# Starting one odd partial sum of a depthwise convolution on TensorE

## The chip, the cores and the metric
The kernel runs on one core of a Trainium2 chip. The metric is the device time in microseconds of one execution; the time given for a kernel is the median of its runs. The core has four engines that compute: TensorE (PE in the profile; PEld is its loading of weights), VectorE (DVE), ScalarE (ACT) and GpSimd (POOL). SyncE (SP) issues the loads. Each engine works through its own instructions in order, and engines meet only at semaphores.

## The reference
Three transformer-like blocks follow one another on 512 tokens of 1024 features. The change touches one place only, the convolution module of the second block:

```python
def conv_module(h, w_in, dw_w, dw_b, ln_g, ln_b, w_out):
    proj = h @ w_in                       # 1024 -> 3 * 2048
    a, b, z = jnp.split(proj, 3, axis=-1)
    u = a * jax.nn.sigmoid(b)
    c = depthwise causal convolution of u with dw_w (31 taps) + dw_b
    ...                                   # norm over 2048 channels, SiLU
    y = jax.nn.silu(cn).astype(h.dtype) * jax.nn.silu(z)
    return y @ w_out
```

For each of the 2048 channels, the output at a token is a sum of 31 taps, each a weight of that channel times `u` at one of the last 31 tokens.

## The kernel before
Features lie on the partitions and tokens along the free axis, so 128 channels by 512 tokens are one channel tile. The 2048 channels are done in eight pairs of channel tiles. A pair needs three weight tiles of 256 output features: its gate `b` (phase 0 or 3), its `a` (phase 1 or 4) and its `z` (phase 2 or 5). A round `i` has two pairs (`h` = 0 and 1, six phases `p`). Rounds 0 to 2 are the segment `seg`: round 0 is written out, rounds 1 and 2 are a loop. Round 3 (`LAST`) is the segment `last`. Below, pairs are counted from 0 to 7.

For every weight tile GpSimd splits the loaded 32-bit weights into a high part (L1406) and a low part (L1412), and TensorE makes 48 products (L1491): 8 blocks of the contraction (`k`), 2 channel tiles (`b`), 3 combinations of high and low parts, in the order k, b, combination. There are two slots for split weights and two accumulators, so the split of a tile waits until TensorE is through with the tile two before it.

The convolution of a pair goes like this:

- `sigmoid` (ScalarE, L2964) turns the accumulated gate into an SBUF tile, after TensorE has finished the gate tile.
- `glu` (VectorE, L2985 to L2988) copies the pair's weights to `wts` and multiplies `a` by the gate into `U`; `half_in` tells ScalarE of the first channel tile, `posted` tells of both.
- `act_products` (ScalarE): taps 6 and 7 begin the even and the odd sum of both channel tiles in PSUM (L2976, four instructions, counted by `begun`). Then taps 0 to 5 go to six SBUF buffers `PROD` (L2981, twelve instructions, counted by `products`).
- `add_half` (GpSimd, L3010) adds these six into `pool_sum`. It is called behind the splits of the next pair's gate and `a` tiles: two additions behind the first, three behind the second, and then `pool_done`. In round 3 the two halves of pair 6 stand behind the splits of phases 3 and 5.
- `conv` (VectorE, L3024): taps 8 to 30, for both channel tiles, each one `scalar_tensor_tensor` that adds a weighted, shifted view of `U` to the even or the odd sum. That is 46 instructions a pair. After each odd tap stands a drain, so that a sum is not read before it is written.
- `finish` (L3032, L3034) waits for `pool_done` and adds the three partial sums.

Pair 7 is done otherwise already, by `conv_last` (L3068): its odd taps 7, 9, 11 and 13 are TensorE's. ScalarE builds for each tap and channel tile a 128x128 diagonal of the weights (`products_last`, L3051), and `tensor_taps` (L3078) multiplies `U` by them within the `z` tile of pair 7, at k = 6. VectorE meanwhile does four even taps, each followed by a drain, and then waits for `tapped`.

Of the kernel before, what the change touches and what calls it, by code (L numbers as in the profile page):

```python
# [19 lines left out]
ACT = mybir.ActivationFunctionType  # L20
AX_X = mybir.AxisListType.X
ds = bass.ds

P = 128
S = 512
# [10 lines left out]
CONV_K = 31  # L36
# [2896 lines left out]
def conv_module_steps(nc, st, w, rhs, rescale):  # L2933


    ctx = ExitStack()
    products, half_in, begun, gate_free, pool_done, going, summed, diagonals_in, tapped = sems(
        nc, ctx, "dw", "products half_in begun gate_free pool_done going summed diagonals tapped")
    pad = CONV_K - 1
    U = st.spare[:, 0:3, :].rearrange("p c n -> p (c n)")[:, 0:2 * (S + 32)].rearrange("p (b n) -> p b n", b=2)  # L2940
    gate = st.spare[:, 3:5, :]
    sums = st.PS[:, 4:8, :]
    halfway = st.spare[:, 5:7, :]
    wts = st.spare[:, 9, 0:2 * CONV_K].rearrange("p (k b) -> p k b", b=2)
    pool_sum = st.spare[:, 10:12, :]

    PROD = (pool_sum, gate, st.spare[:, 12:14, :], st.spare[:, 14:16, :], st.extra[:, :, :], st.A[:, 14:16, :])
    BESIDE = len(PROD)
    LAST = 3
    DIAGONAL = range(BESIDE + 1, BESIDE + 9, 2)  # L2950
    diagonal = lambda b, n: st.spare[:, 7 + b, n * P:(n + 1) * P]
    ADDED = {0: 0, 1: 1, 3: 0, 5: 1}
    dw0 = st.col0["dw0"]
    weights = st.params[:, dw0:dw0 + 16 * CONV_K].rearrange("p (k c) -> p k c", c=16)

    def clear(e):

        for b in range(2):
            e.memset(U[:, b, 0:pad], 0.0)

    def sigmoid(e, acc, i, p):
        e.wait_ge(gate_free, i * 2 + (p // 3 + 1))
        e.sem_inc(going, 1)
        return e.activation(gate, acc, ACT.Sigmoid)  # L2964

    def silu(e, acc, i, p):
        return e.activation(st.A[:, ds(i * 4 + (16 + 2 * (p // 3)), 2), :], acc, ACT.Silu)

    def act_products(e, i, p, posted, begins=2):
        e.wait_ge(half_in, i * 2 + (p // 3 + 1))  # L2970
        for n in range(begins):
            for b in range(2):
                if n == 0 and b == 1:
                    e.wait_ge(*posted)
                k = BESIDE + n
                e.activation(sums[:, 2 * (k % 2) + b, :], U[:, b, k:k + S], ACT.Identity,  # L2976
                             bias=param(st, "conv_dw_b_2", i * 4 + (2 * (p // 3) + b)) if n == 0 else 0.0,
                             scale=wts[:, k, b:b + 1]).then_inc(begun, 1)
        for k in range(BESIDE):
            for b in range(2):  # L2980
                ins = e.activation(PROD[k][:, b, :], U[:, b, k:k + S], ACT.Copy, scale=wts[:, k, b:b + 1])  # L2981
            ins.then_inc(products, 1)

    def glu(e, acc, i, p):
        e.tensor_copy(wts, weights[:, :, ds(i * 4 + 2 * (p // 3), 2)])  # L2985
        e.tensor_tensor(U[:, 0, pad:pad + S], acc[:, 0, :], gate[:, 0, :], ALU.mult)
        e.drain().then_inc(half_in, 1)
        e.tensor_tensor(U[:, 1, pad:pad + S], acc[:, 1, :], gate[:, 1, :], ALU.mult)  # L2988
        return e.drain()

    def add_products(e, i, p):

        first = isinstance(i, int) and i == 0 and p < 3
        if first and p == 2:
            rescale(e)
        if first or p % 3 == 2 or isinstance(i, int) and i == LAST:
            return
        add_half(e, i * 2 + (p // 3 - 1), p % 3)

    def add_products_last(e, i, p):  # L3000

        if i == 0 and p in ADDED:
            add_half(e, 2 * LAST + (p // 3 - 1), ADDED[p])

    def add_half(e, pair, half):
        e.wait_ge(products, pair * BESIDE + (half + 1) * (BESIDE // 2))
        if half == 0:
            e.sem_inc(going, 1)
        for k in range(1, BESIDE // 2) if half == 0 else range(BESIDE // 2, BESIDE):
            ins = e.tensor_tensor(pool_sum, pool_sum, PROD[k], ALU.add)  # L3010
            if k == 1:
                ins.then_inc(gate_free, 1)
            e.drain()
        if half == 1:
            e.drain().then_inc(pool_done, 1)

    def conv(e, i, p):
        h = p // 3
        for k in range(BESIDE + 2, CONV_K):
            for b in range(2):  # L3020
                if k < BESIDE + 4:
                    e.wait_ge(begun, i * 8 + (4 * h + 2 * (k - BESIDE - 2) + b + 1))
                s = sums[:, 2 * (k % 2) + b, :]
                e.scalar_tensor_tensor(s, U[:, b, k:k + S], wts[:, k, b:b + 1], s, ALU.mult, ALU.add)  # L3024
            if k % 2:
                e.drain()  # L3026
        finish(e, i, h)

    def finish(e, i, h):
        e.drain()  # L3030
        e.wait_ge(pool_done, i * 2 + (h + 1))
        e.tensor_tensor(halfway, sums[:, 0:2, :], pool_sum, ALU.add)  # L3032
        e.drain()
        e.tensor_tensor(st.A[:, ds(i * 4 + 2 * h, 2), :], halfway, sums[:, 2:4, :], ALU.add).then_inc(summed, 2)  # L3034

    def phases(first, products_of, conv_of):
        after = lambda act: lambda e, acc, i, p: act(e, acc, i + first, p)
        of = []
        for h in range(2):
            c0 = (2 * first + h) * TW  # L3040
            of += [Phase(D_INNER + c0, act=after(sigmoid), order="gate"),
                   Phase(c0, dve=after(glu), takes=3 * h, more=conv_of, act_more=products_of),
                   Phase(2 * D_INNER + c0, act=after(silu))]
        return of

    def products_last(e, i, p):
        act_products(e, LAST, p, (last.posted, last.posted_at(i, p)), 2 if p < 3 else 1)
        if p < 3:
            for b in range(2):
                for n, k in enumerate(DIAGONAL):  # L3050
                    e.activation(diagonal(b, n), st.ident, ACT.Copy,  # L3051
                                 scale=weights[:, k, 14 + b:15 + b]).then_inc(diagonals_in, 1)

    def conv_last(e, i, p):
        h = p // 3
        if h == 0:
            return conv(e, LAST, p)
        even, odd = ([k for k in range(BESIDE + 2, CONV_K) if k % 2 == n and k not in DIAGONAL] for n in range(2))
        ahead = even[:len(even) - len(odd)]
        rest = [k for pair in zip(odd, even[len(ahead):]) for k in pair]  # L3060
        for at, k in enumerate(ahead + rest):
            for b in range(2):
                if at == 0:
                    e.wait_ge(begun, LAST * 8 + (4 + b + 1))
                if at == len(ahead):
                    e.wait_ge(tapped, b + 1)
                s = sums[:, 2 * (k % 2) + b, :]
                e.scalar_tensor_tensor(s, U[:, b, k:k + S], wts[:, k, b:b + 1], s, ALU.mult, ALU.add)  # L3068
            if at < len(ahead) or k % 2 == 0:
                e.drain()  # L3070
        finish(e, LAST, h)

    def tensor_taps(pe):
        pe.wait_ge(last.posted, last.posted_at(0, 4))
        pe.wait_ge(diagonals_in, 2 * len(DIAGONAL))
        for b in range(2):
            for n, k in enumerate(DIAGONAL):
                mm = pe.matmul(sums[:, 2 + b, :], diagonal(b, n), U[:, b, k:k + S],  # L3078
                               start=(n == 0), stop=(n == len(DIAGONAL) - 1))
            mm.then_inc(tapped, 1)  # L3080

    seg = Seg(w, rhs, LAST, phases(0, lambda e, i, p: act_products(e, i, p, (seg.posted, seg.posted_at(i, p))), conv),
              stride=2 * TW)
    seg.beside = add_products
    last = Seg(w, rhs, 1, phases(LAST, products_last, conv_last))
    last.beside = add_products_last
    last.first_sums = lambda e: add_half(e, 7, 0)
    last.last_sums = lambda e: add_half(e, 7, 1)
    clearing = Part(ctx)
    clearing.vector(clear)  # L3090
    clearing.gpsimd(lambda e: e.nop().then_inc(gate_free, 1))
    last.within = lambda pe, i, p, k: tensor_taps(pe) if (p, k) == (5, 6) else None
    last.chunk_ready = lambda c: (summed, c + 1)
    last.all_posted = lambda: (last.posted, last.posted_at(0, 4))
    return clearing, seg, last
# [614 lines left out]
```

## Time and profile before

| | |
|---|---|
| median of 3 runs | 2593.75 us (2593.53 to 2593.91) |
| the profiled execution, its own time | 2593.49 us |
| its span | 2590.4 us |
| granted TensorE clock, mean | 0.987 |
| busy share of the span | PE 97%, PEld 77%, POOL 60%, DVE 53%, ACT 26% |
| the convolution's pairs, first `glu` to last `finish` | 747.9 to 1039.8 us |
| L3024, instructions and busy time | 322, 220.3 us |
| L3010, instructions and busy time | 40, 95.9 us |

The profile is of one execution. Its span runs from its first to its last instruction, and its own time is 3.1 us longer. The shares are means over a kernel of many stages; what counts for the change is who waits for whom between 748 and 1040 us. The granted clock is TensorE's: 1.00 is 2.4 GHz and 0.50 is 1.2 GHz.

### The profile page before, as it was taken

The numbers are of one execution on the slowest core, as the hardware profiler recorded it, in microseconds if no ns is written. First come the engines' busy times: TensorE is split into PE (matmuls) and PEld (weight loads), VectorE is DVE, ScalarE is ACT, GpSimd is POOL, SyncE is SP. The second block draws the span as 40 slices with busy tenths as digits, with TensorE's granted clock in tenths as the row PEclk, the third lists the DMA queues.
The fourth block names the chain that finished last, engine by engine and source line by source line (L and its number), as shares of the span: only waits on it lengthen the run. The fifth ranks groups of instructions, "written<-read, shape, count | busy, mean of one in ns | idle before, by whom it ended". The sixth has DMA issues, their size and how long they took to land.

```text
span 2590.4 us, 30886 instructions
## 1 busy us (share of the span) xinstructions
PE 2514.1 (97%) x11112; PEld 1991.4 (77%) x11112; DVE 1361.2 (53%) x1915; ACT 668.8 (26%) x1102; POOL 1562.8 (60%) x1061
## 2 busy tenths in 40 slices
PE   7999999999999999999999998999999999999998
PEld 6885588888877776788867886767888777888885
DVE  5996652221379999968214426244356144534345
ACT  3006721100254434421022114133114121300002
POOL 2640257766779898567633765524764467666653
PEclk8999999999999999999999999999999999999999
DMA  9640123333222322133321222311332223223321
GB/s 298 222 157 1 33 67 96 97 98 98 98 82 82 97 81 66 54 98 98 97 81 33 97 84 67 95 50 52 100 93 66 66 81 95 69 96 97 97 80 55
DMA packets 224138, 231.42 MB, mean 89 GB/s; under 512 B 12219, under 2 KB 213788, under 8 KB 223900
## 3 DMA queue, kind: packets, MB, share of 16 engines
q1 hardware_dynamic: 221104, 229.33, 28.0%
q8 instruction: 65, 1.06, 0.2%
q10 hardware_dynamic: 2924, 0.66, 0.1%
q14 instruction: 45, 0.37, 0.0%
HBM read 227.87 MB, written 2.10 MB: 89 GB/s over the span
## 4 chain that ended last, share of the span: by engine, by line
PE 78%; DVE 11%; DVEq 5%; ACT 2%; issue 1%; POOLq 1%; DMA 1%; ACTq 0%; POOL 0%; SPq 0%
PE PS L1491 60%; PE PS L1438 5%; DVE PS L3024 3%; PE PS L1299 3%; DVE A L489 2%; PE PS L2084 1%; DVEq L491 1%; DVEq L3026 1%; PE PS L958 1%; PE PS L2286 1%; PE PS L2303 1%; DVE PS L3068 1%; PE PS L2075 1%; PE PS L2671 1%; DVE X L1066 1%
## 5 line engine op out<-in xcount | busy, mean ns | idle before, releaser
L1412 POOL TENSOR_TENSOR Wl<-raw,Wh 128x512 fp32r<-128x512 f32 (+1 forms) x764 | 1035.3, 1386 | 28.8 <-issue 4.8
L1406 POOL TENSOR_SCALAR Wh<-raw 128x2048 fp32r<-128x2048 f32 (+2 forms) x195 | 366.4, 1880 | 825.3 <-issue 359.0
L1491 PE MATMUL PS<-Hh,Wh 128*128 128x512 f32 x1936 | 765.2, 395 | 33.1 <-POOL Wl L1412 18.1
L1491 PE MATMUL PS<-Hl,Wh 128*128 128x512 f32 x1936 | 759.2, 392 | 0.0
L1491 PE MATMUL PS<-Hh,Wl 128*128 128x512 f32 x1936 | 758.8, 392 | 0.0
L1491 PEld LDWEIGHTS PS<-Hh,Wh 128*128 128x128 f32 x1936 | 366.5, 189 | 120.4 <-POOL Wl L1412 16.1
L1491 PEld LDWEIGHTS PS<-Hh,Wl 128*128 128x128 f32 x1936 | 366.6, 189 | 77.8
L1491 PEld LDWEIGHTS PS<-Hl,Wh 128*128 128x128 f32 x1936 | 366.7, 189 | 77.0 <-issue 1.7
L1491 PE MATMUL PS<-Bh,Wh 128*128 128x512 f32 x688 | 269.3, 391 | 2.6 <-DVE Bl L3320 2.1
L1491 PE MATMUL PS<-Bl,Wh 128*128 128x512 f32 x688 | 267.7, 389 | 0.0
L1491 PE MATMUL PS<-Bh,Wl 128*128 128x512 f32 x688 | 267.7, 389 | 0.0
L3024 DVE SCALAR_TENSOR_TENSOR PS<-spare,PS 128x512 f32<-128x512 f32 x322 | 220.3, 751 | 7.6 <-ACT PS L2976 1.8
L1491 PEld LDWEIGHTS PS<-Bh,Wh 128*128 128x128 f32 x688 | 129.1, 188 | 33.1 <-DVE Bl L3320 3.1
L1491 PEld LDWEIGHTS PS<-Bh,Wl 128*128 128x128 f32 x688 | 129.1, 188 | 27.2
L1491 PEld LDWEIGHTS PS<-Bl,Wh 128*128 128x128 f32 x688 | 129.2, 188 | 26.5 <-issue 0.2
L1594 DVE SCALAR_TENSOR_TENSOR X<-X,PS 128x512 f32<-128x512 f32 (+1 forms) x64 | 41.1, 683 | 160.1 <-PE PS L1491 160.0
L1438 PE MATMUL PS<-Wh,Hh 128*128 128x512 f32 x256 | 100.4, 392 | 1.2 <-DVEq L1385 1.2
L1438 PE MATMUL PS<-Wl,Hh 128*128 128x512 f32 x256 | 99.6, 389 | 0.0
L1438 PE MATMUL PS<-Wh,Hl 128*128 128x512 f32 x256 | 99.6, 389 | 0.0
L1592 DVE SCALAR_TENSOR_TENSOR X<-PS,mod,X 128x512 f32 (+1 forms) x40 | 28.2, 746 | 131.9 <-PE PS L1491 131.9
L2907 DVE SCALAR_TENSOR_TENSOR A<-PS,params,A 128x511 f32 (+5 forms) x116 | 81.5, 744 | 10.1 <-issue 9.0
L2905 DVE TENSOR_SCALAR A<-PS,params 128x512 f32 (+2 forms) x46 | 32.4, 745 | 88.3 <-PE PS L1491 87.8
(497 smaller groups left out, 3009.1 us busy)
## 6 DMA issues: line engine op xcount, KB each, us to landing
raw<-in_w_in SPq DMA_DIRECT2D x44, 1024.0 KB, 5.6
raw<-in_w_ff SPq DMA_DIRECT2D x32, 1024.0 KB, 5.5
raw<-in_conv_w_in SPq DMA_DIRECT2D x24, 1024.0 KB, 5.2
raw<-in_ret_w_in SPq DMA_DIRECT2D x24, 1024.0 KB, 5.1
spare<-in_ada_w SPq DMA_DIRECT2D x20, 1024.0 KB, 7.7
raw<-in_w_up SPq DMA_DIRECT2D x20, 1024.0 KB, 5.4
raw<-in_w_out SPq DMA_DIRECT2D x8, 1024.0 KB, 5.2
raw<-in_conv_w_out SPq DMA_DIRECT2D x8, 1024.0 KB, 5.1
```

The costliest lines, as they stand in the source:

```text
L489: dve.scalar_tensor_tensor(a, tile[:, k, :], silu_c[:, k:k + 1], a, ALU.mult, ALU.add)
L491: dve.drain()
L1299: mm = pe.matmul(acc[0:m, b, :], w[:, k, b * P:b * P + m], x[:, k, :], start=(k == 0 and n == 0), stop=(k == KC - 1 and n == 2))
L1406: pool.tensor_scalar(st.Wh[0:rows, slot, k, 0:cols], st.raw_slot(slot)[0:rows, k, 0:cols], 1.0, 1.0, ALU.mult, ALU.mult)
L1412: ins = pool.tensor_tensor(st.Wl[0:rows, slot, k, 0:cols], st.raw_slot(slot)[0:rows, k, 0:cols], st.Wh[0:rows, slot, k, 0:cols].bitcast(F3 ...
L1438: mm = pe.matmul(st.PS[:, b, :], x[:, p * HALF_K + k, b * P:(b + 1) * P], w[:, k, :], start=(p == 0 and k == 0 and n == 0), stop=(p == 1 a ...
L1491: mm = pe.matmul(out, lhs, rhs, start=(k == parts[0][0] and n == 0), stop=(k == parts[-1][0] and n == 2))
L1592: ins = e.scalar_tensor_tensor(x, a, gate[:, ds(i * 4 + (2 * p + b), 1)], x, ALU.mult, ALU.add)
L1594: ins = e.scalar_tensor_tensor(x, x, x_scale, a, ALU.mult, ALU.add)
L2905: ins = e.tensor_scalar(out[0:m, b, :], acc[0:m, b, :], w, None, ALU.mult)
L2907: ins = e.scalar_tensor_tensor(out[0:m, b, back:S], acc[0:m, b, 0:S - back], w, out[0:m, b, back:S], ALU.mult, ALU.add)
L3024: e.scalar_tensor_tensor(s, U[:, b, k:k + S], wts[:, k, b:b + 1], s, ALU.mult, ALU.add)
```

## The change
In pairs 0 to 6 the odd sum of the second channel tile (b = 1) is begun by TensorE and not by ScalarE. ScalarE builds two 128x128 diagonals of that tile's weights, for taps 7 and 9, behind the gate's sigmoid and ahead of its wait for `half_in`. TensorE multiplies `U` by them into `sums[:, 3, :]`, two 32-bit products within the pair's `z` tile, at k = 4, after waits for the diagonals and for `posted`. ScalarE's tap 7 of b = 1 goes, and so does VectorE's tap 9 of b = 1.

VectorE's taps are put in another order: even taps 8, 10 and 12 first, each followed by a drain; then nine pairs of an odd and an even tap (9 and 14, 11 and 16, ... 25 and 30), with a drain after each; then taps 27 and 29, each with a drain. The wait for TensorE's product (`tapped`) stands at tap 11 of b = 1. Pair 7 is as before but for the counts of the semaphores, which change for everyone.

```diff
@@ conv_module_steps
+    BEGIN, AHEAD = (BESIDE + 1, BESIDE + 3), 3
+    begin_diagonal = lambda n: st.spare[:, 9, (1 + n) * P:(2 + n) * P]
...
-    def act_products(e, i, p, posted, begins=2):
+    def act_products(e, i, p, posted, looped=True):
+        if looped:
+            for n, k in enumerate(BEGIN):
+                e.activation(begin_diagonal(n), st.ident, ACT.Copy,
+                             scale=weights[:, k, ds(i * 4 + (2 * (p // 3) + 1), 1)]).then_inc(diagonals_in, 1)
         e.wait_ge(half_in, i * 2 + (p // 3 + 1))
-        for n in range(begins):
-            for b in range(2):
+        for n, b in ((0, 0), (0, 1), (1, 0)) if looped else ((0, 0), (0, 1)):
...
     def conv(e, i, p):
         h = p // 3
-        for k in range(BESIDE + 2, CONV_K):
+        even, odd = ([k for k in range(BESIDE + 2, CONV_K) if k % 2 == n] for n in range(2))
+        pairs = [k for pair in zip(odd, even[AHEAD:]) for k in pair]
+        for at, k in enumerate(even[:AHEAD] + pairs + odd[len(even) - AHEAD:]):
             for b in range(2):
-                if k < BESIDE + 4:
-                    e.wait_ge(begun, i * 8 + (4 * h + 2 * (k - BESIDE - 2) + b + 1))
+                if k == BEGIN[1] and b == 1:
+                    continue
+                if at == 0:
+                    e.wait_ge(begun, i * 6 + (3 * h + b + 1))
+                if k == odd[0]:
+                    e.wait_ge(begun, i * 6 + (3 * h + 3))
+                if k == odd[1] and b == 1:
+                    e.wait_ge(tapped, i * 2 + (h + 1))
                 s = sums[:, 2 * (k % 2) + b, :]
                 e.scalar_tensor_tensor(s, U[:, b, k:k + S], wts[:, k, b:b + 1], s, ALU.mult, ALU.add)
-            if k % 2:
+            if k % 2 == 0 or at >= AHEAD + len(pairs):
                 e.drain()
         finish(e, i, h)
+
+    def tensor_begin(pe, posted, i, h):
+        pe.wait_ge(diagonals_in, i * 4 + (2 * h + 2))
+        pe.wait_ge(*posted)
+        for n, k in enumerate(BEGIN):
+            mm = pe.matmul(sums[:, 3, :], begin_diagonal(n), U[:, 1, k:k + S], start=(n == 0), stop=(n == 1))
+        mm.then_inc(tapped, 1)
...
-        act_products(e, LAST, p, (last.posted, last.posted_at(i, p)), 2 if p < 3 else 1)
+        act_products(e, LAST, p, (last.posted, last.posted_at(i, p)), p < 3)
...
-                    e.wait_ge(begun, LAST * 8 + (4 + b + 1))
+                    e.wait_ge(begun, LAST * 6 + (3 + b + 1))
                 if at == len(ahead):
-                    e.wait_ge(tapped, b + 1)
+                    e.wait_ge(tapped, LAST * 2 + 1 + b + 1)
...
-        pe.wait_ge(diagonals_in, 2 * len(DIAGONAL))
+        pe.wait_ge(diagonals_in, LAST * 4 + 2 + 2 * len(DIAGONAL))
...
-    last.within = lambda pe, i, p, k: tensor_taps(pe) if (p, k) == (5, 6) else None
+    seg.within = lambda pe, i, p, k: (tensor_begin(pe, (seg.posted, seg.posted_at(i, p - 1)), i, p // 3)
+                                      if (p % 3, k) == (2, 4) else None)
+    last.within = lambda pe, i, p, k: (tensor_taps(pe) if (p, k) == (5, 6) else
+                                       tensor_begin(pe, (last.posted, last.posted_at(0, 1)), LAST, 0)
+                                       if (p, k) == (2, 4) else None)
```

## Rows read from the trace of the kernel before
**Rows 1.** Busy time by stretch (windows), one pair of the loop; columns as PE, PEld, DVE, ACT, POOL, clock.
```profile
859.00:896.00 37.00, 34.34 (x146) 28.01 (x145) 35.39 (x52) 14.81 (x20) 32.77 (x21) 0.96 0.27 86
```
**Rows 2.** Waits between 745 and 1060 us: waiter, releaser, total us, times, longest.
```profile
ACT PS L2976 <- DVEq L2987: 94.3, 8, 15.8
...
PE PS L1491 <- POOL Wl L1412: 18.1, 7, 3.7
...
POOL spare L3010 <- ACT spare L2981: 13.3, 6, 2.5
```
**Rows 3.** Timeline of VectorE, pair 1 and the start of pair 2: start, length.
```profile
784.58 0.26 DVE L2985 COPY spare<-params 128x62 f32<-128x62 f32 x1
...
786.45 32.30 DVE L3024 SCALAR_TENSOR_TENSOR PS<-spare,PS 128x512 f32<-128x512 f32 x46 [0.21 <-ACT PS L2976]
...
821.26 0.21 DVE L2985 COPY spare<-params 128x62 f32 x1
```
**Rows 4.** The chain that ended last, in order of time: pair 0, first four taps.
```profile
749.78 2.07 DVE PS L3024 x3
...
752.59 0.76 DVE PS L3024
```
**Rows 5.** Timeline of VectorE: pair 6's finish, pair 7's taps.
```profile
1004.05 1.22 DVE L3032 TENSOR_TENSOR spare<-PS,spare 128x1024 f32<-128x1024 f32 x1 [0.88 <-POOLq L3015]
...
1008.37 6.73 DVE L3068 SCALAR_TENSOR_TENSOR PS<-spare,PS 128x512 f32<-128x512 f32 x9 [0.21 <-ACT PS L2976]
1015.42 21.71 DVE L3068 SCALAR_TENSOR_TENSOR PS<-spare,PS 128x512 f32<-128x512 f32 x31 [0.32 <-PE PS L3078]
```
**Rows 6.** Timeline of ScalarE: two begins of a pair, and eight diagonals.
```profile
787.02 1.29 ACT L2976 ACTIVATE PS<-spare 128x512 f32<-128x512 f32 x2
...
980.04 2.44 ACT L3051 ACTIVATE spare<-squares,params 128x128 f32<-128x128 f32 x8
```
**Rows 7.** Timeline of TensorE: pair 7's eight diagonal products, and the second product behind them.
```profile
1008.25 7.13 PE L3078 MATMUL PS<-spare 128*128 128x512 f32 x16
...
1015.45 0.39 PE L1491 MATMUL PS<-Hl,Wh 128*128 128x512 f32 x1
```
**Rows 8.** Timeline of TensorE: first and last products of stretches without a wait.
```profile
758.44 0.79 PE L1491 MATMUL PS<-Hh,Wh 128*128 128x512 f32 x1 [3.72 <-POOL Wl L1412]
...
782.95 0.39 PE L1491 MATMUL PS<-Hh,Wl 128*128 128x512 f32 x1
785.57 0.50 PE L1491 MATMUL PS<-Hh,Wh 128*128 128x512 f32 x1 [2.24 <-POOL Wl L1412]
...
818.12 0.39 PE L1491 MATMUL PS<-Hh,Wl 128*128 128x512 f32 x1
820.23 0.47 PE L1491 MATMUL PS<-Hh,Wh 128*128 128x512 f32 x1 [1.72 <-POOL Wl L1412]
...
856.40 0.58 PE L1491 MATMUL PS<-Hh,Wh 128*128 128x512 f32 x1 [3.25 <-POOL Wl L1412]
...
890.55 0.39 PE L1491 MATMUL PS<-Hh,Wl 128*128 128x512 f32 x1
...
967.13 0.50 PE L1491 MATMUL PS<-Hh,Wh 128*128 128x512 f32 x1 [2.29 <-POOL Wl L1412]
```
**Rows 9.** Busy time by stretch, the first 5.8 us behind TensorE's longest wait.
```profile
758.40:764.20 5.80, 5.76 (x14) 4.50 (x15) 5.65 (x9) 2.93 (x4) 5.36 (x3) 0.50 0.56 182
```
**Rows 10.** Timeline of GpSimd: splits and additions of pairs 1, 4 and 6.
```profile
765.59 5.02 POOL L1412 TENSOR_TENSOR Wl<-raw,Wh 128x512 fp32r<-128x512 f32 x4
...
780.51 5.00 POOL L1412 TENSOR_TENSOR Wl<-raw,Wh 128x512 fp32r<-128x512 f32 x4
...
902.85 2.41 POOL L3010 TENSOR_TENSOR spare<-spare 128x1024 f32<-128x1024 f32 x1 [2.47 <-ACT spare L2981]
...
989.38 1.91 POOL L1406 TENSOR_SCALAR Wh<-raw 128x2048 fp32r<-128x2048 f32 x1 [0.35 <-issue]
...
1001.51 2.39 POOL L3010 TENSOR_TENSOR spare<-spare,A 128x1024 f32<-128x1024 f32 x1
```

## The prediction
> **What bounds the kernel now.** I read the times first, then the busy time by stretch over the convolution's pairs, then the waits in it, and last the timelines of the four engines. The page alone misleads: TensorE is 97% busy over the kernel, but within a loop pair VectorE is busy 35.4 of 37 us, GpSimd 32.8 and TensorE 34.3 [rows 1]. All three are close to the bound. The timeline settles which one leads. VectorE goes from one pair's copy to the next in 821.26 - 784.58 = 36.68 us with no wait worth the name [rows 3]. TensorE waits for GpSimd's split some 2.6 us a pair, GpSimd waits for ScalarE's products up to 2.5 us a pair, and ScalarE waits for VectorE's `glu` [rows 2]. So in the loop VectorE leads, its `glu` paces ScalarE, ScalarE paces GpSimd's additions, and GpSimd paces TensorE's `z` tile.
>
> The end of the stage is different, and it decides what arrives. In pair 6 GpSimd starts the split of the last `z` tile at 989.38, after a short wait [rows 10]. It was held by TensorE: the first of pair 6's `z` products starts at 967.13 [rows 8], and the 96 products of `z` and the next gate take two thirds of the 32.78 us that 144 take at full clock (818.12 - 785.57, and 0.23 for the last) [rows 8]. That is 967.13 + 21.9 = 989.0. The additions behind this split end at 1001.51 + 2.39 = 1003.9 [rows 10], and only then can VectorE finish pair 6, after waiting 0.88 us [rows 5]. In pair 7 VectorE waits again for TensorE's diagonal products, 0.32 us [rows 5]. From 967 us on the end is set by TensorE's path.
>
> **The change part by part.**
>
> *VectorE.* Four taps in a group with one drain take 752.59 - 749.78 = 2.81 us [rows 4]. In pair 7, four groups of two and one single fill 6.73 us, the single being 0.76 [rows 4, 5], so a group of two takes 1.49. The two differ by 1.32, which is 0.66 us for one instruction, and 1.49 - 1.32 leaves 0.17 for a drain. Before, a pair has 46 instructions and 11 drains between them: 46 x 0.66 + 11 x 0.17 = 32.2, and the row has 32.30 [rows 3]. After, it has 45, and 3 + 9 + 1 = 13 drains between them (the last one merges with `finish`'s). It gains 0.66 - 2 x 0.17 = 0.32 us a pair. The two ends for this are 0 and 0.66.
>
> The rows say that a drain costs 0.17 us [rows 4, 5]. The Trainium skill, "VectorE: DVE Perf Modes", section "Rules for kernel authors", says that a pipeline flush follows every VectorE operation in any case and that one should count operations, not semaphores. By that rule drains are free and a pair gains 0.66, but VectorE also comes to its new wait 1.0 us sooner; the sum below would then be 2594.2. These rows do not bear it out, for a group of two is dearer per instruction than one of four.
>
> *ScalarE.* One of four begins goes, 1.29 / 2 = 0.6 us [rows 6], so the products that GpSimd waits for come 0.6 earlier after `glu`. Two diagonals are added, 2 x 2.44 / 8 = 0.6 us [rows 6]. They stand ahead of the wait for `glu`, which is 94.3 us in 8 waits [rows 2], so they cost nothing. Without that cover they would cost 0.6 a pair.
>
> *TensorE.* From 1008.25 to 1015.45 there are eight diagonal products and two ordinary ones; 7.20 - 2 x 0.23 = 6.74, or 0.84 each [rows 7]. Two cost 1.7 us a pair (1.8 if all of the 7.13 is theirs). In the loop the full-clock work becomes 32.8 + 1.7 = 34.5 of 36.4 us, so VectorE still leads and the wait for GpSimd hides it. For pair 6 nothing hides it: there it lies on the path from 967 us on.
>
> *The new wait of VectorE.* In a pair, tap 11 of b = 1 is reached after three groups of two, one group of three and one single: 3 x 1.49 + (3 x 0.66 + 0.17) + 0.66 = 7.3 us after the first tap. Behind it are queued all other taps, `finish` and the next `glu`, and then ScalarE and GpSimd. TensorE's product comes (5.5 + 1.7) us after the start of the `z` tile at full clock (24 of 144 products, a sixth of 32.8). For pair 2, that is 820.23 + 7.2 = 827.4 [rows 8]; VectorE asks at some 830.5 (its taps start 1.9 us after the copy [rows 3]), so there is no wait. Pair 1 is the one to look at.
>
> *Pair 1.* Its `z` tile starts at 785.57 because GpSimd's split of it ends at 780.51 + 5.00 = 785.5 [rows 8, 10]. GpSimd is late there for its own reasons, and the change does not move this. Before, TensorE idled 3.72 us ahead of the gate tile at 758.44, and the granted clock stood at 0.50 for the next 5.8 us [rows 8, 9], which is 1.2 GHz. That gate tile and the `a` tile behind it took 24.7 us (782.95 - 758.44 + 0.23) in place of 21.9, so the low clock cost 2.9. Elsewhere an idle 3.25 us cost 34.4 - 32.8 = 1.6, and 1.72 us and 2.24 us cost nothing [rows 8].
>
> With the change, pair 0's `z` tile takes in the two products, with a short wait for `posted` of about 0.6. It fills 2.3 of the 3.7 idle us, and the gate tile should run at full clock. It then ends at 769.3, the `a` tile follows when its split is in at 765.59 + 5.02 = 770.6 [rows 10], and it ends at 781.6. TensorE now idles 785.5 - 781.6 = 3.9 us ahead of pair 1's `z` tile. So the idle time, and the low clock behind it, moves from a place where it hurt nobody to one just ahead of the new product. I take the clock to cost between 1.6 and 2.9 us there. The product is in at 785.57 + 5.5 + 1.7 + (1.6 to 2.9) = 794.4 to 795.7. VectorE asks at 786.45 - 0.3 + 7.3 = 793.4. It stalls 1.0 to 2.3 us, once; I take 1.6. Nothing gives this back, for VectorE leads from there on.
>
> *The sum.* Pair 6's `z` tile starts when its split is in, and that follows pair 5's `glu` through ScalarE and GpSimd (as the waits of 2.5 us show [rows 2, 10]). It moves by -5 x 0.32 (pairs 0 to 4) - 0.6 (ScalarE) + 1.6 (stall in pair 1) = -0.6. The products within it add 1.7. The gate's end, GpSimd's last `z` split, `pool_done`, pair 6's `finish` and pair 7's taps all come 1.1 us later. VectorE's own pair 6 is ready earlier, so its wait for GpSimd grows from 0.9 to some 2.5 us. What follows pair 7 hangs on its `finish`, so the 1.1 us reach the end. The span becomes 2591.5, the profiled execution's own time 2593.49 + 1.1 = 2594.6, and the median, which is 0.26 above that execution, 2594.9.
>
> **The rivals.**
>
> *No stall.* If TensorE keeps its clock in pair 1, the product is in at 792.8, ahead of VectorE. The sum is then -1.6 - 0.6 + 1.7 = -0.5, 2593.3. For it: 2.24 us idle did no harm. Against it: 3.72 and 3.25 did [rows 8].
>
> *The whole of VectorE's gain arrives.* If the path through TensorE at the end has slack that I do not see, the stage ends 7 x 0.32 earlier and without the wait of 0.88: -3.1, 2590.6. Against it: the waits at 1004 and 1015 [rows 5]. If the added drains cost nothing either, it would be 7 x 0.66 + 0.88 = 5.5, at 2588.3, the only way to a gain above 0.2%.
>
> *TensorE becomes the bound.* If it idles and drops its clock in each pair, and the new products fall into the low spell, its work is 32.8 + 2.9 + 3.4 (twice 1.7) = 39.1 us a pair, and VectorE is held at tap 11 every time. Against 36.7 that is +2.4 over pairs 1 to 6, 14 us: 2608. It decides from about 0.9 us a pair upwards. Against it: with 34.5 us of work the idle time shrinks to some 2 us, and the low spells seen before end within 5.8 us of the tile's start.
>
> **How the numbers follow.** 0.2%, or 5.2 us, is about what a measurement of this kernel can tell from no change. The forecast (a stall once, a little later at the end) has 0.57, no stall 0.20, VectorE's gain arriving 0.15, the same with drains that cost nothing 0.03, TensorE the bound 0.05. The range for 8 in 10 goes from 2590.5, which takes in VectorE's gain arriving, to 2597.5, which holds the longest stall and diagonal products of 1.8 with no gain from the taps (+2.3 + 1.8 - 0.6 = 3.5, 2597.3). Faster by over 0.2% has 0.03, slower 0.04, within it 0.93.
>
> **What would show it.** VectorE's taps of a loop pair should last 32.0 us and not 32.3, at 45 instructions. In pair 1 the line of the taps should wait 1.0 to 2.3 us for TensorE's product, and in pairs 2 to 6 not at all. The clock should be low behind 785 and high behind 758. Pair 6's `finish` should wait over 2 us for GpSimd. The forecast is wrong in its mechanism if waits for `tapped` come in other pairs, if a loop pair's period is not 36.4 us, or if pair 7's taps do not start 1 us later than 1008.4.

## The result and the profile after
The changed kernel takes 2598.89 us (median of 17 runs, 2594.16 to 2602.65) against 2593.53 us for the kernel before (17 runs, 2590.05 to 2596.85). The ratio is 1.0022, with a 95% interval of 1.0015 to 1.0029; by the medians the change is 5.4 us slower. (Here and below, a ratio and its interval are worked out from all runs of both kernels. They are not the quotient of the two medians, and a difference read from one can lie up to 1.6 us from that read from the other.) The forecast was 2594.9 with a range up to 2597.5, so the result lies outside it.

The profiled execution took 2596.03 us, with a span of 2594.2. Below, "the stage" is the stretch from VectorE's copy of pair 0's weights to the norm's first subtraction (the line after `finish` of pair 7). It lasts 291.94 us before (747.93 to 1039.87) and 293.37 after (746.07 to 1039.44): 1.4 us more, where 1.1 was forecast. So this one profile seems to bear the forecast out while the median does not. The study is about that gap.

The timeline of VectorE in the changed kernel (start, length, idle time before it and its releaser), pairs 1, 2, 3 and 6, answers to [rows 3, 5]:
```profile
782.46 0.25 DVE L2990 COPY spare<-params 128x62 f32<-128x62 f32 x1
...
784.33 7.39 DVE L3037 SCALAR_TENSOR_TENSOR PS<-spare,PS 128x512 f32<-128x512 f32 x10 [0.21 <-ACT PS L2981]
792.53 24.68 DVE L3037 SCALAR_TENSOR_TENSOR PS<-spare,PS 128x512 f32<-128x512 f32 x35 [0.81 <-PE PS L3046]
...
821.93 15.07 DVE L3037 SCALAR_TENSOR_TENSOR PS<-spare,PS 128x512 f32<-128x512 f32 x21 [0.29 <-ACT PS L2981]
837.43 16.92 DVE L3037 SCALAR_TENSOR_TENSOR PS<-spare,PS 128x512 f32<-128x512 f32 x24 [0.43 <-issue]
...
858.96 32.09 DVE L3037 SCALAR_TENSOR_TENSOR PS<-spare,PS 128x512 f32<-128x512 f32 x45 [0.28 <-ACT PS L2981]
...
972.37 28.97 DVE L3037 SCALAR_TENSOR_TENSOR PS<-spare,PS 128x512 f32<-128x512 f32 x41 [0.45 <-issue]
1003.64 1.22 DVE L3052 TENSOR_TENSOR spare<-PS,spare 128x1024 f32<-128x1024 f32 x1 [2.29 <-POOLq L3020]
```
Pair 1 stops after ten taps, at tap 11 of b = 1, and waits 0.81 us for TensorE. Pair 6's `finish` waits 2.29 us for GpSimd, where it waited 0.88. Pairs 2 and 6 have a break of over 0.4 us that waits for nothing the profile shows.

The chain that ended last, in pair 1 (start, length, what), and TensorE's timeline at the start of the `z` tiles of pairs 1 and 6, which answers to [rows 8]:
```profile
783.73 7.05 PE PS L1491 x24
790.78 1.72 PE PS L3046 x4
```
```profile
783.73 0.80 PE L1491 MATMUL PS<-Hh,Wh 128*128 128x512 f32 x1 [3.67 <-POOL Wl L1412]
...
964.92 0.50 PE L1491 MATMUL PS<-Hh,Wh 128*128 128x512 f32 x1 [1.92 <-POOL Wl L1412]
```
The two diagonal products take 1.72 us. The 24 products ahead of them take 7.05 us and not the forecast's 5.5, since the clock is low at first. In pair 6, where it is not, the same chain has 5.73:
```profile
964.92 5.73 PE PS L1491 x24
```
So 5.5 was itself some 0.25 us short, and the low clock costs 1.3 in pair 1. The busy time by stretch (bounds, length, busy time of PE, PEld, DVE, ACT and POOL, then the granted clock, the share of DMA and GB/s) shows the low clock behind pair 1's start and not behind pair 6's:
```profile
783.70:787.00 3.30, 3.27 (x9) 2.63 (x10) 3.01 (x5) 3.27 (x6) 3.15 (x3) 0.57 0.55 172
...
964.90:970.50 5.60, 5.58 (x25) 4.62 (x26) 5.02 (x7) 2.42 (x4) 5.45 (x4) 1.00 0.57 187
```
GpSimd's wait for ScalarE's products, 2.47 us before [rows 10], is shorter in its timeline:
```profile
900.80 2.42 POOL L3015 TENSOR_TENSOR spare<-spare 128x1024 f32<-128x1024 f32 x1 [2.14 <-ACT spare L2986]
```

### The profile page after: what moved, and what is told of

Same layout as the page of the kernel before. It is cut to its first block, busy times and chain, and to the rows that moved or that the text cites. A ratio compares the mean times of both kernels' runs of the same rounds, so it can differ in the third digit from the quotient of the medians.

```text
span 2594.2 us, 30978 instructions
## 1 busy us (share of the span) xinstructions
PE 2521.6 (97%) x11140; PEld 1990.4 (77%) x11140; DVE 1355.5 (52%) x1908; ACT 669.3 (26%) x1109; POOL 1563.8 (60%) x1061
## 4 chain that ended last, share of the span: by engine, by line
PE 79%; DVE 9%; DVEq 4%; ACT 2%; POOLq 1%; POOL 1%; issue 1%; DMA 1%; ACTq 0%; SPq 0%
PE PS L1491 61%; PE PS L1438 5%; PE PS L1299 3%; DVE A L489 2%; PE PS L2084 1%; DVEq L491 1%; POOLq L3018 1%; DVE PS L3037 1%; PE PS L958 1%; PE PS L2286 1%; PE PS L2303 1%; POOL Wl L1412 1%; DVE PS L3088 1%; PE PS L2075 1%; DVEq L526 1%
```

## The experiments

### More executions of both kernels
`again`, the changed kernel with nothing edited:

> The changed kernel as it is, for a second profile and more times. Theory A (the forecast's path: the stage itself loses 1 to 2 us, one stall in pair 1 and 1.7 us on TensorE's path in pair 6, and the rest of the 5.4 us is TensorE's clock falling at other places in some executions): the stage from pair 0's copy of weights to the norm's first subtraction lasts 293 to 294 us against 291.9 before, and the whole is 1 to 6 us over the kernel before, from execution to execution. Theory B (something outside the stage became slower for good, as code loading would make it): the stage is as under A, and the same stretch outside it is again 2 us or more longer than in the kernel before.

`control`, the kernel before with nothing edited:

> The kernel before once more, as a control. Both theories: ratio 1.000 within its interval. Theory A: its profile differs from the first one by 1 to 3 us outside the convolution stage, at places where TensorE's granted clock is at 0.50 in one and 1.00 in the other. Theory B: outside the stage the two profiles agree within 0.5 us.

`again` has a median of 2600.23 us (11 runs) against 2593.45 (33 runs), ratio 1.0021 (1.0012 to 1.0031). `control` has 2593.83, ratio 1.0001 (0.9992 to 1.0010). The stage in `control` is again 291.95 us, but in `again` it is 296.59. VectorE's timeline of `again`, in pairs 1 and 6:
```profile
784.86 7.39 DVE L3037 SCALAR_TENSOR_TENSOR PS<-spare,PS 128x512 f32<-128x512 f32 x10 [0.21 <-ACT PS L2981]
794.64 2.90 DVE L3037 SCALAR_TENSOR_TENSOR PS<-spare,PS 128x512 f32<-128x512 f32 x4 [2.40 <-PE PS L3046]
...
1007.38 1.23 DVE L3052 TENSOR_TENSOR spare<-PS,spare 128x1024 f32<-128x1024 f32 x1 [3.88 <-POOLq L3020]
```
The stall is 2.40 us in place of 0.81, and pair 6 waits 3.88 in place of 2.29. TensorE's timeline shows the same idle times as in the first profile, and the stretches behind them a clock that stays low longer in pair 1 and falls in pair 6 as well:
```profile
784.25 0.79 PE L1491 MATMUL PS<-Hh,Wh 128*128 128x512 f32 x1 [3.68 <-POOL Wl L1412]
...
967.06 0.50 PE L1491 MATMUL PS<-Hh,Wh 128*128 128x512 f32 x1 [1.93 <-POOL Wl L1412]
```
```profile
784.20:790.70 6.50, 6.46 (x16) 5.06 (x17) 6.05 (x10) 6.47 (x11) 6.35 (x5) 0.52 0.48 161
...
967.00:972.00 5.00, 4.94 (x15) 3.90 (x16) 4.49 (x7) 1.78 (x3) 4.85 (x5) 0.66 0.66 210
```
The chain that ended last, in pair 1 of `again`, puts what the stall has grown by down to the clock: 24 products take 8.64 us, 2.9 more than the 5.73 at full clock, and the diagonal ones 1.72 as before.
```profile
784.25 8.64 PE PS L1491 x24
792.89 1.72 PE PS L3046 x4
```
In pair 6 of `again` the chain's 24 products take 7.36 us, against 5.73 in the first profile. GpSimd's split of the last `z` tile, which is held until TensorE is through the next gate tile, shows it on the path: it starts 25.64 us after pair 6's `z` tile (992.70 - 967.06), where it started 24.01 after it in the first profile (988.93 - 964.92) and 22.25 before the change (989.38 - 967.13 [rows 8, 10]). The first step, 1.8 us, is the two products; the second, 1.6 us, is the clock.
```profile
967.06 7.36 PE PS L1491 x24
```
```profile
992.70 1.92 POOL L1406 TENSOR_SCALAR Wh<-raw 128x2048 fp32r<-128x2048 f32 x1 [3.77 <-issue]
```
Theory A expected 293 to 294 us of stage, so it was wrong in this; theory B, with a fixed loss outside the stage, explains none of the 4.6 us that are inside it. Theory A also expected `control` to differ from the first profile by 1 to 3 us outside the stage; it differs by 0.5. Three more profiles of the changed kernel and one of the kernel before were taken to see how often it is so.

> A further profile of the changed kernel. The theory of the two low clocks: the stage is 293.4 us with the short stall in pair 1 and no fall in pair 6, up to 1.6 us more for the longer stall, and 1.6 more for a fall in pair 6, so that it lies between 293.4 and 296.6.

> A further profile of the kernel before. The stage is again 291.9 to 292.0 us, whatever the clock did in it, since its low spells lie where TensorE waits anyway; behind the stage it lasts 1550.5 to 1555 us, the differences lying at falls of the clock.

> A further profile of the changed kernel. Stage between 293.4 and 296.6 us; with the long stall in pair 1 and the fall ahead of pair 6 (296.6) if the time is near 2600, with the short stall and no fall (293.4) if it is near 2595.

> The same once more: 296.6 us of stage at a time near 2600, 293.4 at one near 2595.

| kernel | execution's time | stage | stall in pair 1 | pair 6, copy to copy | clock falls ahead of pair 6 |
|---|---|---|---|---|---|
| before | 2593.49 | 291.94 | none | 37.44 | no |
| control | 2592.99 | 291.95 | none | 37.44 | no |
| control_2 | 2592.12 | 292.01 | none | 37.50 | no |
| changed | 2596.03 | 293.37 | 0.81 | 38.90 | no |
| again | 2601.59 | 296.59 | 2.40 | 40.50 | yes |
| again_2 | 2600.71 | 296.60 | 2.45 | 40.48 | yes |
| again_3 | 2592.89 | 292.29 | none | 38.93 | no |
| again_4 | 2596.04 | 296.11 | 1.94 | 40.50 | yes |

The expectation of 293.4 to 296.6 held for `again_2` and `again_4`; `again_3` fell below it, with no stall at all. (`control_2` came out as expected.) In pair 1 of `again_3` TensorE idled 3.69 us and kept its clock, by its timeline and the stretch behind:
```profile
782.78 0.50 PE L1491 MATMUL PS<-Hh,Wh 128*128 128x512 f32 x1 [3.69 <-POOL Wl L1412]
```
```profile
783.00:787.00 4.00, 4.00 (x18) 3.27 (x18) 3.63 (x6) 3.97 (x7) 3.85 (x3) 1.00 0.73 229
```
So the kernel before has one length of stage and the changed kernel several, from 292.3 to 296.6.

The kernel before has falls of the clock too. In all three of its profiles the granted clock is 0.72 in the 6 us behind the starts of the `z` tiles of pairs 3, 4 and 5, after idle times of some 3.2, 2.6 and 2.2 us. This is the stretch behind pair 5's, where TensorE had idled 2.18 us:
```profile
930.31:936.31 6.00, 6.00 (x19) 4.82 (x20) 5.42 (x9) 3.19 (x5) 5.85 (x5) 0.72 0.53 175
```
There the falls cost nothing, for VectorE leads and waits for nothing of TensorE's. But this trace was at hand before the forecast, and it shows a fall behind an idle time as short as those of 2.24 and 2.29 us that kept the clock. The pairing of `again_4` (296.1 at 2596.04, not at 2600) also says that the time outside the stage varies by some us.

### Keeping TensorE busy ahead of pair 1
```diff
@@ weights_part, tensor
+                if g.fill and isinstance(i, int) and (i, p) == g.fill[0]:
+                    pe.wait_ge(freed[slot], turn + 1)
+                    keep_busy(pe, st, acc_of(slot)[:, 0, :], g.fill[1])
                 if not (g.by_pairs and p == 0):
                     pe.wait_ge(split_done, t + SLOTS + 1)
@@ conv_module_steps
+    seg.fill = ((0, 5), 12)
```

> The changed kernel with 12 products of constants (2.8 us) ahead of TensorE's wait for the split of pair 1's z tile. If the low clock there causes the stall at tap 11: the granted clock behind the tile's start is 1.00, the stall of 0.8 us in pair 1 goes, and the stage is 0.8 us shorter (up to 2.3 in executions with a longer low spell). Rival: the stall comes from GpSimd's late split alone, and stays.

The median is 2595.39 us (11 runs, 2594.72 to 2597.05) against 2593.45, ratio 1.0010 (1.0001 to 1.0019): 4.8 us less than `again` on the same chip by the medians, 2.9 by the ratios. In its profile the stage is 292.48. VectorE's 45 taps of pair 1 run without a break, 31.98 us, and the clock behind the start of the `z` tile is 1.00 (timeline, then the stretch):
```profile
785.67 31.98 DVE L3041 SCALAR_TENSOR_TENSOR PS<-spare,PS 128x512 f32<-128x512 f32 x45 [0.21 <-ACT PS L2985]
```
```profile
785.00:788.00 3.00, 2.91 (x13) 2.41 (x14) 2.71 (x5) 2.97 (x5) 2.85 (x3) 1.00 0.50 144
```
The split of pair 1's `z` tile is as late as ever, so the rival, that GpSimd alone makes the stall, falls. By the medians more came back than the 2.4 us of the longest stall. In this profile TensorE also idles only 0.5 us ahead of pair 6, since its clock is low through part of pair 5 (0.77), where it does no harm; so `fill` took away the falls at both places, and does not say what each was worth.
```profile
928.50:936.00 7.50, 7.50 (x25) 5.93 (x26) 6.76 (x10) 4.27 (x7) 6.86 (x5) 0.77 0.43 140
```

### Pair 6 and the path to the end
`pair6_before` takes the change out of pair 6 alone:
```diff
-        act_products(e, LAST, p, (last.posted, last.posted_at(i, p)), p < 3)
+        act_products(e, LAST, p, (last.posted, last.posted_at(i, p)), 'four' if p < 3 else False)
...
         if h == 0:
-            return conv(e, LAST, p)
+            for k in range(BESIDE + 2, CONV_K):
+                for b in range(2):
+                    if k < BESIDE + 4:
+                        e.wait_ge(begun, LAST * 6 + (2 * (k - BESIDE - 2) + b + 1))
+                    s = sums[:, 2 * (k % 2) + b, :]
+                    e.scalar_tensor_tensor(s, U[:, b, k:k + S], wts[:, k, b:b + 1], s, ALU.mult, ALU.add)
+                if k % 2:
+                    e.drain()
+            return finish(e, LAST, 0)
...
-    last.within = lambda pe, i, p, k: (tensor_taps(pe) if (p, k) == (5, 6) else
-                                       tensor_begin(pe, (last.posted, last.posted_at(0, 1)), LAST, 0)
-                                       if (p, k) == (2, 4) else None)
+    last.within = lambda pe, i, p, k: tensor_taps(pe) if (p, k) == (5, 6) else None
```

> Pair 6 alone is as in the kernel before (four begins on ScalarE, 46 taps in the old order, no TensorE product in its z tile); pairs 0 to 5 are changed. Forecast's path: the stage ends 1.7 us earlier than in the changed kernel, 291.5 to 292 us long, and VectorE's wait for GpSimd in pair 6 falls from 2.3 to about 1 us. If that path does not set the end: no difference in the stage, or a longer one by the 0.66 us tap.

The median is 2598.93 (11 runs) against 2593.45, ratio 1.0023 (1.0014 to 1.0032), no clear gain over `again`. In its profile the stage is 294.37 with a stall of 1.91 in pair 1, and pair 6 takes 38.74 us with a wait for GpSimd of 2.17, where about 1 was expected. The expectation had not thought of the clock. TensorE's timeline at the start of pair 6's `z` tile, the stretch around it, GpSimd's timeline at the split that waits for this tile's successor, and VectorE's `finish`:
```profile
965.84 0.54 PE L1491 MATMUL PS<-Hh,Wh 128*128 128x512 f32 x1 [1.93 <-POOL Wl L1412]
```
```profile
964.00:970.00 6.00, 4.17 (x11) 3.30 (x12) 5.35 (x8) 1.00 (x2) 5.85 (x5) 0.72 0.50 161
```
```profile
989.70 1.92 POOL L1406 TENSOR_SCALAR Wh<-raw 128x2048 fp32r<-128x2048 f32 x1 [1.65 <-issue]
```
```profile
1004.40 1.23 DVE L3052 TENSOR_TENSOR spare<-PS,spare 128x1024 f32<-128x1024 f32 x1 [2.17 <-POOLq L3020]
```
The clock falls there without the two products too, behind 1.93 us of idle time, and GpSimd's split then waits 1.65 us where it waited 0.35 [rows 10]. So pair 6's path is what was forecast, and a low clock on it costs what the products had cost. Kernels with fillers take the two apart. `fill_both` adds products of constants ahead of pair 6's `z` tile to `fill`; `fill_both_pair6` is both fillers with the edit of `pair6_before`, and was taken twice; `fill_pair6` is that without this line:
```diff
     last.beside = add_products_last
+    last.fill = ((0, 2), 6)
```

> The changed kernel with 12 products of constants ahead of the z tile of pair 1 and 6 (1.4 us) ahead of the z tile of pair 6. The theory now: what the changed kernel loses beyond 0.5 us in the stage is TensorE's low clock at two places, behind its 3.7 us idle ahead of pair 1 (stall of 0.8 to 2.4 us at tap 11) and, in some executions, behind its 1.9 us idle ahead of pair 6 (1.6 us more). Then the stage is 292.5 us or less in every profile, the median 2594 to 2595.5, and the spread is that of the fill kernel (2.3 us) or less. Rival: pair 6 never mattered, and the times are those of the fill kernel.

> As fill_both, but pair 6 is as in the kernel before, so that no product of TensorE's lies on the path that ends the stage. If VectorE's gain in pairs 0 to 5 and ScalarE's begin are real (0.2 to 0.3 us a pair and 0.6), the stage is 290.6 to 291.2 us, about 1 us shorter than in the kernel before, and the median is 2592.5 to 2593.5. If the gain was never there, 291.9 or more.

> The changed kernel with pair 6 as before and products of constants ahead of pair 1's z tile alone, none ahead of pair 6's. If pair 6's filler mattered: the stage is 290.7 us in some executions and 1.6 more in others, and the median lies 0.5 to 1.5 us over that of the kernel with both fillers (2591.9). If not, it equals it.

> The kernel with both fillers and pair 6 as before, once more, to tell whether it beats the kernel before. The theory of the stage: 290.7 us against 291.9, and a ratio of 0.9988 to 0.9998. Rival: the first measurement was luck at the clock's falls, and the ratio is 1.000 or above.

| kernel | median | before, same chip | ratio (95%) | stage | pair 6, copy to copy |
|---|---|---|---|---|---|
| fill_both | 2595.42 | 2593.43 | 1.0006 (0.9997 to 1.0015) | 292.20 | 38.85 |
| fill_both_pair6 | 2591.87 | 2593.43 | 0.9990 (0.9981 to 0.9999) | 290.73 | 37.17 |
| fill_both_pair6_2 | 2593.54 | 2594.92 | 0.9996 (0.9987 to 1.0005) | 290.75 | 37.17 |
| fill_pair6 | 2593.44 | 2594.92 | 0.9988 (0.9979 to 0.9997) | 290.73 | 37.07 |

VectorE's timeline of `fill_both_pair6` in pairs 6 and 7 shows what the two products had cost:
```profile
1002.88 1.23 DVE L3056 TENSOR_TENSOR spare<-PS,spare 128x1024 f32<-128x1024 f32 x1 [0.60 <-POOLq L3024]
...
1007.19 6.73 DVE L3100 SCALAR_TENSOR_TENSOR PS<-spare,PS 128x512 f32<-128x512 f32 x9 [0.21 <-ACT PS L2985]
1014.43 2.07 DVE L3100 SCALAR_TENSOR_TENSOR PS<-spare,PS 128x512 f32<-128x512 f32 x3 [0.50 <-PE PS L3110]
```
With the clock high at both places, taking the products out of pair 6 shortens the stage by 292.20 - 290.73 = 1.5 us, near the 1.72 that they take. And it leaves a kernel whose stage is 1.2 us shorter than before. The three measurements of such kernels have ratios of 0.9988 to 0.9996; two of the three intervals end below 1, the third does not. So it is probably faster than the kernel before, by some 1.5 us by the medians and 1.0 to 3.1 by the ratios, which is little more than the measurement tells. The expectation for `fill_pair6` was missed where it gave pair 6's filler a price: neither stage nor median differs from `fill_both_pair6_2` on the same chip, so nothing here shows that this filler is needed. `fill_both` met its 292.5 but not its narrower spread (2592.47 to 2596.95).

### A later end of the stage, and nothing else
Both are the kernel before with copies ahead of pair 7's last additions (2 or 6):
```diff
@@ finish
         e.drain()
+        for _ in range(2 if isinstance(i, int) and i == LAST and h == 1 else 0):
+            e.tensor_copy(halfway[:, 0, :], sums[:, 0, :])
+            e.drain()
```

> The kernel before, with two copies of 512 columns and a drain behind each ahead of pair 7's last additions: nothing but 1.5 us of delay at the end of the stage, 293.4 to 293.6 us. Question: does the delay of the stage alone change what TensorE's clock does behind it? If it does not (the clock's falls behind the stage are a lottery that is the same for every kernel), the median rises by 1.5 us, to 2595. If the later end itself moves the falls to dearer places, as the changed kernels' profiles suggest (2 to 4 us more behind the stage), it rises by 3.5 to 5 us.

> The same with six copies: 4.7 us of delay, which is what the changed kernel lost in the stage in two of three profiles. Without an effect on the clock behind the stage the median rises by 4.7, to 2598.2; with one by more than 6 or less than 3.5 us.

`delay_2` has a stage of 293.51 us (+1.6) and a median of 2596.95 against 2594.92 (+2.0), ratio 1.0008 (0.9999 to 1.0017). `delay_6` has a stage of 296.53 (+4.6) and 2600.42 against 2594.92 (+5.5), ratio 1.0026 (1.0016 to 1.0037). The second is the changed kernel's case made by hand: the stage is as long as in `again` (296.59), and the ratio is as that of `again` (1.0021) and of the change (1.0022), within the intervals. A stage that is 4.6 us longer is enough for a median that is 5.4 us higher. An excess of 0.4 and 0.9 us over the delay itself is within the intervals; the large effect on what lies behind the stage that the first expectation allowed for is not there.

### The order of the taps alone
`order_alone` keeps VectorE's new order and drains. ScalarE begins all sums, VectorE has all 46 taps, and TensorE's two products are left out in pairs 0 to 6 (the edit against the changed kernel, without the counts of the semaphores):
```diff
-        if looped:
+        if False:
             for n, k in enumerate(BEGIN):
...
-        for n, b in ((0, 0), (0, 1), (1, 0)) if looped else ((0, 0), (0, 1)):
+        for n, b in ((0, 0), (0, 1), (1, 0), (1, 1)) if looped else ((0, 0), (0, 1)):
...
-                if k == BEGIN[1] and b == 1:
-                    continue
...
-                if k == odd[1] and b == 1:
-                    e.wait_ge(tapped, i * 2 + (h + 1))
...
-    seg.within = lambda pe, i, p, k: (tensor_begin(pe, (seg.posted, seg.posted_at(i, p - 1)), i, p // 3)
-                                      if (p % 3, k) == (2, 4) else None)
```

> VectorE's new order of taps and drains alone: ScalarE begins all four sums, VectorE has all 46 taps, and TensorE's two products and their diagonals are left out in pairs 0 to 6. By the rows' price of a drain (0.17 us) a pair's taps last 32.3 + 2 x 0.17 = 32.6 us and the stage 2 to 2.7 us longer than before, 294 to 294.7. By the rule that added drains are free: 32.3 us a pair and 291.9. TensorE's clock in pair 1 then is as in the kernel before (idle ahead of pair 1's gate tile), with no stall at tap 11.

The median is 2598.09 against 2594.95, ratio 1.0014 (1.0005 to 1.0023), and the stage 296.12, longer than expected. VectorE's timeline, pair 1:
```profile
787.70 32.64 DVE L3033 SCALAR_TENSOR_TENSOR PS<-spare,PS 128x512 f32<-128x512 f32 x46 [0.21 <-ACT PS L2981]
```
32.64 against 32.30 [rows 3] are the 0.34 us of two more drains. From copy to copy pairs 0 and 1 take 0.4 us more and the loop's pairs 2 to 5 some 0.47. Of the 4.2 us in the stage these are 2.6; pair 6 takes 1.2 more, and the clock falls ahead of it (0.71 in the stretch below, behind 2.8 us of idle time), and pair 7 takes 0.3 more: VectorE stands still for 0.44 us ahead of the norm's first subtraction, for nothing the profile shows.
```profile
970.10:976.00 5.90, 5.84 (x19) 4.63 (x20) 5.02 (x7) 2.55 (x4) 5.75 (x6) 0.71 0.56 179
```
Two drains a pair cost half of the 0.66 us that the tap taken out is worth.

## Why the prediction was wrong, step by step
- **Which engine leads, and how the waits hang together: right.** The stage's time went where the chain said: a stall in pair 1, pair 6's `finish` behind GpSimd, pair 7 moved with it. The waits for `tapped` come in pair 1 only. The forecast's own sign of a wrong mechanism, a loop pair's period other than 36.4 us, did come: pairs 2 to 5 take 36.71 to 37.00. Part of that is a misreading. The 36.68 us that it starts from is pair 1, in the round that is written out; the loop's pairs took 36.92 to 36.98 before.
- **VectorE's taps: right in size, short in effect.** A pair's taps take 31.98 us against 32.30, the 0.32 that was forecast. But copy to copy, in the profile of the change, pairs 0, 2, 3 and 4 gain 0.26, -0.08, 0.27 and 0.17, and pair 1, its wait of 0.81 taken off, loses 0.06. Together that is 0.6 us and not 5 x 0.32 = 1.6. Two parts of it were not in the sum: breaks of 0.43 us in pair 2 and 0.19 in pair 4 (and 0.45 in pair 6), and that a stall costs 0.3 us beyond its wait, since `fill`'s pair 1 takes 36.42 and the stalled one 37.55 with a wait of 0.81.
- **The rule on drains.** The Trainium skill, "VectorE: DVE Perf Modes", section "Rules for kernel authors", tells to count operations and not semaphores, since the flush comes in any case. Read as "added drains are free", as the forecast's rival did, it would have had 0.66 us a pair. The taps of `order_alone` contradict that reading: two more drains, 0.34 us more. The section does not speak of drain instructions that a kernel adds.
- **ScalarE's saved begin: right.** From the copy to GpSimd's first addition it is 900.80 - 893.72 = 7.08 us, against 902.85 - 895.16 = 7.69.
- **The two products: right.** 1.72 us, and 1.5 to 1.8 on the path to the end (`fill_both` against `fill_both_pair6`; from pair 6's `z` tile to the end of the stage 74.52 us against 72.74).
- **The idle time that moves ahead of pair 1's `z` tile: right, but taken as one number.** 3.9 us was forecast, 3.67 measured. The stall was taken as 1.6 (1.0 to 2.3); five profiles have 0, 0.81, 1.94, 2.40 and 2.45. The two longest lie outside the bounds: the low clock cost 2.9 us, as the forecast's upper bound had it, but the 24 products take 5.73 at full clock and not 5.5.
- **The step that failed** is "from 967 us on the end is set by TensorE's path", with its 21.9 us for 96 products at full clock. I had looked at the clock only where idle time grows. Ahead of pair 6 it shrinks (1.9 us against 2.29 [rows 8]), so I took the full clock for granted. In three of five profiles it falls there (0.66 in `again`), and pair 6 takes 1.6 us more, straight on the path that the change has just made longer. This term stood at nothing, on the strength of idle times of 1.72, 2.24 and 2.29 us that kept the clock; pair 5's 2.18 us, which did not, was not read.
- **The sum for an execution like `again`.** The stage is 4.65 us longer where 1.1 was forecast. Of the 3.5 us between them the fall ahead of pair 6 is 1.6, the stall in pair 1 is 1.1 (2.7 with what it costs beyond its wait, against 1.6), and the taps are 0.8 (a gain of 0.8 in pairs 0 to 4, the stall's own price counted above, and not 1.6). So the fall is the largest term, and alone it is less than half. Three of the five profiles have both spells, and `delay_6` shows that 4.6 us of stage make a median that is 5.5 higher.
- **The range** ended at 2597.5, made of the longest stall and no gain from the taps, without a fall at pair 6. With it, it would have ended at 2599.1 and held the median.

Two things stay open. What decides whether the clock falls in an execution: the kernel before idled 2.23 to 2.29 us ahead of pair 6 without a fall in three of three profiles, the changed one 1.9 us with a fall in three of five (and `pair6_before` once more), the kernel before idled 2.18 to 2.27 us ahead of pair 5 with a fall in three of three, and idle times of 3.67 to 3.69 ahead of pair 1 were followed by a short spell, a long one or none. And the time outside the stage: execution less stage is 2300.1 to 2301.6 us in three executions of the kernel before and 2299.9 to 2305.0 in five of the changed one, which may add to the median beyond the stage. From the end of the stage to the end of the span it is 1550.5 to 1552.0 us in those three and 1553.6 to 1556.6 in those five, but `delay_2`, `delay_6` and `order_alone`, whose ends are late as well, have 1553.5, 1554.5 and 1551.3. Why is not shown.

## What to carry to other kernels
Work that is put into another engine's idle time moves that idle time; ask where it goes, and whether something new waits just behind it. One profile is one execution: where a path runs over TensorE right behind an idle time, take several profiles before believing a difference of a few us. And taking an instruction out of a chain of dependent sums is worth less than its duration when the new order needs more drains.

## What the runs showed of the hardware
- The same idle time of TensorE (3.67 to 3.69 us) was followed by a granted clock of 1.00, by a spell that cost 1.3 us, and by longer ones that cost up to 2.9 (24 products in 7.05 and 8.64 us, against 5.73 at a clock of 1.00).
- The length of the idle time alone did not tell whether the clock falls: behind 2.18 to 2.27 us it was 0.72 in three of three profiles (pair 5, kernel before), behind 2.23 to 2.29 us 1.00 in three of three (pair 6, kernel before), and behind 1.9 us 0.72 in three of five (pair 6, changed kernel).
- Twelve small products of constants in such an idle time, 2.8 us, kept the clock at 1.00 in pair 1 in all five profiles of kernels with them (`fill` and the four others); without them one of six kept it (five of the changed kernel and `pair6_before`). The median of `fill` is 4.8 us below that of `again`.
- A drain on VectorE between dependent 128x512 operations costs 0.17 us, worked out in two ways (groups of two against four before, and `order_alone`).
